# Attention heads unrolled across loop borders, three-pass scores in two mixers, and no staged queries

## The reference

```python
def _nsa(q, kc_raw, vc_raw, ks, vs, kw, vw, gates, ...):        # 8 heads, 2 key groups, HD = 64
    kc = _compress(kc_raw, pos_k, ck_w1, ck_w2)                 # 31 compressed keys
    vc = _compress(vc_raw, pos_v, cv_w1, cv_w2)
    ...
        s_c = jnp.einsum('bqghd,bngd->bghqn', qc, kc) * scale
        p_c, _ = _probs(s_c, cmp_end[None, :] <= t[:, None])
        o_c = jnp.einsum('bghqn,bngd->bqghd', p_c, vc)
        ...                                                     # o_s: selected blocks, o_w: window
        return gc[..., 0:1] * o_c + gc[..., 1:2] * o_s + gc[..., 2:3] * o_w

def _dilated_mixture(q, k, v): ...                              # 8 heads, HD = 64, one mask with weights
def _mla_mixer(...):                                            # 16 heads
        sc = (einsum('bqhd,bkhd->bhqk', qn, k_nope) + einsum('bqhr,bkr->bhqk', qr, k_rope)) * scale
        p, _ = _probs(sc, k_pos[None, :] <= t[:, None])
        return jnp.einsum('bhqk,bkhd->bqhd', p, v)

def _gqa(q, k, v):                                              # 8 heads of 128, 2 key groups, 768 keys
    s = jnp.einsum('bqkgd,bskd->bkgqs', q, k) * (ATTN_HEAD_DIM ** -0.5)
    p = jax.nn.softmax(s, axis=-1)
    return jnp.einsum('bkgqs,bskd->bqkgd', p, v)
```

## Time and profile before

| what | value |
|---|---|
| median of 3 runs | 3901.3 us (3901.02 to 3901.65) |
| profiled execution | 3896.48 us, its span 3894.7 us |
| PE busy | 3483.3 us (89%) |
| DVE busy | 2051.7 us (53%) |
| ACT busy | 1229.4 us (32%) |
| POOL busy | 271.5 us (7%) |
| chain that ended last | PE 77%, DVE 12%, ACT 3%, POOL 2% |
| share of the chain in `three` (L759 to L761) | 66% |
| compress stage, from 629.93 to 681.05 us | 51.12 us |
| `nsa` and `dil`, to 865.50 us | 184.45 us |
| `mla`, 1821.09 to 1938.50 us | 117.41 us |
| `attn`, 3292.74 to 3447.65 us | 154.91 us |

### The profile page before, as it was taken

How to read it: one execution, slowest core, us unless ns; L and a number is a source line. 1 busy time by engine, 2 the same in 40 slices (tenths; PEclk the granted TensorE clock), 3 DMA queues, 4 the chain that set the end, 5 groups by cost and what they waited for, 6 DMA issues and landing times.

```text
span 3894.7 us, 47690 instructions
## 1 busy us (share of the span) xinstructions
PE 3483.3 (89%) x16433; PEld 2822.0 (72%) x16433; DVE 2051.7 (53%) x2953; ACT 1229.4 (32%) x1890; POOL 271.5 (7%) x258
## 2 busy tenths in 40 slices
PE   8999988889999999988999994498899875778999
PEld 6888767567888788865678883398688753566887
DVE  7743433555753675355555435675655356335553
ACT  3222311443222322233532222454333232323332
POOL 1000111001000100022010003300000011000000
PEclk9999995999999999888999997599899987998999
DMA  5533240003542354211045420265233210012332
GB/s 170 171 94 98 88 109 1 0 7 112 168 124 81 109 171 124 81 59 33 1 118 167 124 92 27 59 172 163 76 97 102 91 65 22 1 43 76 97 103 70
DMA packets 390883, 347.27 MB, mean 89 GB/s; under 512 B 11344, under 2 KB 343437, under 8 KB 390669
## 3 DMA queue, kind: packets, MB, share of 16 engines
q1 hardware_dynamic: 390797, 346.16, 29.8%
HBM read 344.02 MB, written 2.10 MB: 89 GB/s over the span
## 4 chain that ended last, share of the span: by engine, by line
PE 77%; DVE 12%; issue 4%; ACT 3%; POOL 2%; SPq 1%; DMA 0%; DVEq 0%; ACTq 0%; POOLq 0%
PE ps L759 22%; PE ps L760 22%; PE ps L761 22%; PE ps L850 3%; PE ps L824 2%; POOL sq_sum L2147 2%; PE ps L1244 1%; ACT w_hi L1297 1%; DVE w_lo L1310 1%; DVE a_lo L1635 1%; DVE rstd L1658 1%; PE ps L841 1%; DVE x_T L2131 1%; PE ps L821 1%; PE ps L957 1%
## 5 line engine op out<-in xcount | busy, mean ns | idle before, releaser
L759 PE MATMUL ps<-a_hi,w_hi 128*128 128x512 f32 (+1 forms) x2968 | 1144.7, 386 | 135.5 <-DVE a_lo L1901 42.7
L760 PE MATMUL ps<-a_lo,w_hi 128*128 128x512 f32 (+1 forms) x2968 | 1130.6, 381 | 0.0
L761 PE MATMUL ps<-a_hi,w_lo 128*128 128x512 f32 (+1 forms) x2968 | 1130.0, 381 | 0.0
L759 PEld LDWEIGHTS ps<-a_hi,w_hi 128*128 128x128 f32 x2968 | 570.8, 192 | 281.4 <-issue 114.6
L1310 DVE TENSOR_TENSOR w_lo<-w_raw,w_hi 128x1024 fp32r<-128x1024 f32 (+1 forms) x536 | 636.3, 1215 | 183.3 <-ACT w_hi L1297 169.4
L1297 ACT ACTIVATE w_hi<-w_raw 128x1024 fp32r<-128x1024 f32 (+1 forms) x536 | 549.8, 1044 | 308.5 <-PE ps L761 306.7
L761 PEld LDWEIGHTS ps<-a_hi,w_lo 128*128 128x128 f32 x2968 | 571.6, 193 | 103.8
L760 PEld LDWEIGHTS ps<-a_lo,w_hi 128*128 128x128 f32 x2968 | 572.5, 193 | 100.8 <-issue 1.0
L759 PE MATMUL ps<-hs_hi,w_hi 128*128 128x512 f32 (+1 forms) x1232 | 464.9, 377 | 2.8 <-DVE w_lo L1310 1.5
L760 PE MATMUL ps<-hs_lo,w_hi 128*128 128x512 f32 (+1 forms) x1232 | 463.7, 376 | 0.0
L761 PE MATMUL ps<-hs_hi,w_lo 128*128 128x512 f32 (+1 forms) x1232 | 463.3, 376 | 0.0
(11 more groups left out here) (250 smaller groups left out, 3251.5 us busy)
## 6 DMA issues: line engine op xcount, KB each, us to landing
w_raw<-in_ffn_w_up SPq DMA_DIRECT2D x220, 512.0 KB, 4.8
w_raw<-in_ffn_w_down SPq DMA_DIRECT2D x154, 512.0 KB, 3.5
ada_raw<-in_ada_w SPq DMA_DIRECT2D x96, 512.0 KB, 3.9
w_raw<-in_ffn_w_gate SPq DMA_DIRECT2D x88, 512.0 KB, 5.1
w_raw<-in_ev_w_in SPq DMA_DIRECT2D x20, 512.0 KB, 3.6
w_raw<-in_attn_w_qkv SPq DMA_DIRECT2D x16, 512.0 KB, 4.2
w_raw<-in_ev_w_out SPq DMA_DIRECT2D x8, 512.0 KB, 4.1
w_raw<-in_mla_w_out SPq DMA_DIRECT2D x8, 512.0 KB, 3.2
```

The lines of the kernel that those rows point to most:

```text
L759: mm(dst, hi, rhi, start=start, stop=False)
L760: mm(dst, hi, rlo, start=False, stop=False)
L761: return mm(dst, lo, rhi, start=False, stop=stop)
```

## The change

1. **Unrolled units.** `attention` on PE, ACT and DVE walks all units in straight code. PE's order per unit u and step j is: scores(u+1, next tile), transposes(u, j+1), values(u, j), across the old iteration borders too. At the last step the first transpose of u+1 stands ahead of the last values of u.
2. **ACT's order.** A `take` of step j now stands ahead of the exponentials of unit u+1 that it stood between or behind: `attn` has take, exp instead of exp, take; the causal mixers have take 1, exp 0, exp 1, take 3, exp 2, exp 3.
3. **Scale.** The softmax scale, with its sign turned, is multiplied into the queries where they are made (and into the gains of `mla` and `attn`); the masks change sign, DVE takes minima, and the exponential has scale -1 and that minimum as its bias. L1690 and a wait between DVE and ACT go.
4. **No staging.** POOL's copies and the `stage` tiles go. Scores read queries and keys in place: 64 rows of `F` in `nsa` and `dil`, 96 in `mla`, 128 in `attn`.
5. **Three-pass scores** in `nsa`, `dil` and `attn`: ACT makes the high part of a 128x512 tile (`qk_hi`), DVE the rest (`qk_lo`). In the even mixer 14 tiles: 7 inside the rope loop, 7 (`later`) one in each of `nsa`'s units 0 to 6. In `attn` 10: 4 before the first unit, 6 one in each of units 0 to 5. On DVE `qk_lo` stands between the last maximum of u+1 and `finish(u)`. `mla` keeps one float32 matmul.
6. **Compress** has no loop: scores of two heads in one three-pass matmul of 64 columns (48 matmuls), softmax on 4 heads at a time (two groups of 128x512), 8 transposes, 8 float32 value matmuls of 256 columns with block-diagonal values.

The core of the diff:

```diff
+            ph.cmp.step0 = dve_step.plan(12)
+
+            def pair(f, rows):
+                return F_hi(f)[rows, :], F_r[rows, f, :]
+
+            def head(f_q, f_k, side, v, out, need, gate=None):
+                rows = slice(HD * side, HD * side + HD)
+                return dict(q=pair(f_q, rows), k=pair(f_k, rows), v=v, out=out, gate=gate, need=ph.qk0 + need)
+
+            heads = []
+            for it in range(4):
+                for branch in range(2):
+                    for side in range(2):
+                        gate = it * 3 + 12 * side + 1 + branch
+                        heads.append(head(it, 6 + 2 * branch, side,
+                                          lambda kb, b=branch, s=side: v_tok[:, kb, b, HD * s:HD * s + HD],
+                                          o_tok[:, :, it * HD + 256 * side:it * HD + 256 * side + HD], 6,
+                                          gates[:, :, gate:gate + 1]))
+            ph.nsa = attention_plan(heads, "causal", work=work_even, mask=masks[:, 0, :], dim=HD,
+                                    later=[[(F[:, f, :], F_hi(f), F_r[:, f, :])] for f in SPLIT[7:]])
...
+            splits, heads = [], []
+            for i in range(2):
+                splits.append((k_att[:, i, :], k_att_hi[:, i, :], k_att_lo[:, i, :]))
+                for u in range(4):
+                    h = 4 * i + u
+                    splits.append((q_att[:, h, :], q_att_hi[:, h, :], q_att_lo[:, h, :]))
+                    heads.append(dict(q=splits[-1][1:], k=splits[5 * i][1:], v=lambda kb, i=i: v_att[:, kb, i * P:i * P + P],
+                                      out=o_att[:, :, h * P:h * P + P], gate=None, need=ph.qk0 + len(splits)))
+            ph.first_splits = splits[0:4]
+            ph.att = attention_plan(heads, "full", work=work_att, mask=zeros[:, :], dim=P, later=[[x] for x in splits[4:]])
...
+                ring = 2 if full else 4
+                units_t = [(c, range(3 * h, 3 * h + 3)) for c in range(4) for h in range(2)] if full else \
+                    [(c, range(c + 1)) for c in range(4)]
+
+                def scores(u, c):
+                    head = at.heads[u]
+                    if c == 0 and head["need"] is not None:
+                        pe.wait_ge(qk_lo_s.sem, head["need"])
+                    if 4 * u + c >= ring:
+
+                        pe.wait_ge(sm_s.sem, at.sm0 + 4 * u + c - ring + 1)
+                    parts = [(0, 512, 2 * (c % 2)), (512, 768, 2 * (c % 2) + 1)] if full else [(0, (c + 1) * P, c)]
+                    for first, end, bank in parts:
+                        dst = ps[:, bank, 0:end - first]
+                        q = [t[:, c * P:(c + 1) * P] for t in head["q"]]
+                        k = [t[:, first:end] for t in head["k"]]
+                        if len(q) == 2:
+                            last = three(dst, q[0], q[1], k[0], k[1], True, True)
                         else:
-                            last = mm(ps[:, c, 0:(c + 1) * P], q, at.k(it, u, (c + 1) * P), start=True, stop=True)
...
+                def turn_(u, j):
+                    c, kbs = units_t[j]
...
+                def values(u, j):
+                    c, kbs = units_t[j]
+                    made, first = ((ptd_s, at.ptd0), (pta_s, at.pta0))[j % 2]
+                    pe.wait_ge(made.sem, first + per_t // 2 * u + j // 2 + 1)
+                    if j == 0 and u >= 2:
...
+                for c in range(4):
+                    scores(0, c)
+                for u in range(at.units):
+                    if u == 0:
+                        turn_(0, 0)
                     for j in range(per_t):
-
-                        if u < 3 and j % (per_t // 4) == 0:
-                            scores(u + 1, it, (j // (per_t // 4),))
+                        if u + 1 < at.units and j % (per_t // 4) == 0:
+                            scores(u + 1, j // (per_t // 4))
                         if j + 1 < per_t:
-                            turn_(j + 1)
...
-                with pe.Fori(0, at.units // 4) as it:
-                    scores(0, it)
-                    for u in range(4):
-                        rest(u, it)
...
+                    for it in range(4):
+                        for c in range(4):
+                            tok = slice(c * P, (c + 1) * P)
+                            dst = ps[:, it // 2, :].rearrange("p (i s c n) -> p i s c n", i=2, s=2, c=4)[:, it % 2, :, c, :]
+                            last = three(dst, F_hi(it)[:, tok], F_r[:, it, tok], kc_hi[:, :], kc_lo[:, :], True, True)
...
+            def qk_hi(split):
+                do(split[1], split[0], ACT.Copy).then_inc(qk_hi_s.sem, 1)
+
...
-                def rest(u, it):
-                    for j in range(per_t):
-                        if u < 3 and j % (per_t // 4) == 0 and j % 2 == 0:
-                            exps(u + 1, it, (j // (per_t // 4),))
-                        if j % 2 == 0:
-                            continue
-                        act.wait_ge(t_s.sem, v_at(at.t0 + per_t * u + j + 1, it, 4 * per_t))
-                        if j >= 2:
-                            act.wait_ge(pv_s.sem, v_at(at.pv0 + per_t * u + j - 1, it, 4 * per_t))
-                        width = 384 if full else (j + 1) * P
-                        do(wk.pT[:, 1, 0:width], ps[:, 5, 0:width], ACT.Copy).then_inc(pta_s.sem, 1)
-                        if u < 3 and not full:
...
+                for c in range(4):
+                    exps(0, c)
+                for u in range(at.units):
+                    more = u + 1 < at.units
+                    for j in range(1, per_t, 2):
+                        take(u, j)
+                        for c in ((j // 2,) if full else (j - 1, j)) if more else ():
+                            exps(u + 1, c)
+                    for split in at.later[u] if u < len(at.later) else ():
+                        qk_hi(split)
...
+            def qk_lo(split, n):
+                src, hi, lo = split
+                dve.wait_ge(qk_hi_s.sem, n + 1)
+                v.tensor_tensor(lo, src, hi.bitcast(F32), ALU.subtract).then_inc(qk_lo_s.sem, 1)
...
-                            v.tensor_scalar(NM[:, u % 2, c:c + 1], MX[:, u % 2, c:c + 1], -at.scale, None, ALU.mult)\
-                             .then_inc(nm_s.sem, 1)
...
+                for c in range(4):
+                    maxima(0, c)
+                for u in range(at.units):
+                    more = u + 1 < at.units
+                    for j in range(0, per_t, 2):
+                        take(u, j)
+                        for c in ((j // 2,) if full else (j, j + 1)) if more else ():
+                            maxima(u + 1, c)
+                    for split in at.later[u] if u < len(at.later) else ():
+                        qk_lo(split, split0 + nsplit[0])
+                        nsplit[0] += 1
+                    finish(u)
...
+                        if 3 <= r <= 9:
+                            f = ROPED[r - 2]
+                            qk_lo((F[:, f, :], F_hi(f), F_r[:, f, :]), ph.qk0 + r - 3)
...
-            def stage_queries(at):
-
-
-                stage = at.work.stage
-                with pool.Fori(0, at.units // 4) as it:
-                    for u in range(at.stages):
-                        q, side = at.q(it, u)
-                        rows = slice(0, at.rows) if side is None else slice(HD * side, HD * side + HD)
-
-                        pool.wait_ge(s_s.sem, v_at(at.s0 - 16 + 4 * (u + 1 if at.stages == 4 else u + 3), it, 16))
-                        g.tensor_copy(stage[rows, u, :].unsqueeze(1), q[rows]).then_inc(st_s.sem, 1)
```

505 lines of the change are left out of this document (244 added, 261 removed).

## The result

The changed kernel takes 3929.95 us (median of 4 runs, 3925.06 to 3935.03) against 3901.16 (3899.97 to 3901.65): a ratio of 1.0074, 95% interval 1.0057 to 1.0092, so 28.8 us slower. The profiled execution took 3930.02 us, 33.5 more than the one of before. Later executions of the kernel before took 3884 to 3927 us (3884 to 3907 in nine on one chip); none of them is traced, so which stage makes this spread isn't known.

What follows compares the result with a forecast made beforehand. PE, busy 89% of the span and holding 77% of the chain, was taken as the bound. Compress -23.6, attn -38, mla -12, nsa and dil +84, projection +2.3 gave +12.7: 3914 us on the median, range 3828 to 3930.

Steps and rivals of the forecast that it cites:

- nsa and dil: Stages nsa and dil: clock at 0.50 throughout, units of 12.2, 10.8 and 10.3 us, +84 us (+72 to +92).
- the term for mla: Stage mla: ACT's wait goes, units of 6.4 instead of 7.1 us, -12 us (-2 to -14).
- Rival 3: Low clock reaches mla too: five units stay there at 5.4 us more each, kernel 3941 us; chance 0.05.
- One of my own signs: Forecast is wrong if three passes of 512 columns on 64 rows take over 0.7 us at full clock.
- The start of nsa: nsa was to start at 1.2 GHz, since compress stays there.
- the sign of rival 1: Whether the clock comes up in nsa and dil is decided in the first 10 us of nsa.
- rival 1: Clock comes up in nsa and dil as now: 169 to 192 us there, kernel 3825 us; chance 0.18.
- the reason given: nsa and dil: the one thing in a unit after which the clock rose, 128-row float32 scores, is taken out.
- attn: Stage attn: take ahead of exp ends ACT's wait, tile 3.12 us, split waits 10 us in all; -38 us (-30 to -41).
- Compress: Stage compress: batched matmuls and softmax, 51.1 to 27.5 us, -23.6 us (-18 to -30).
- Projection: Output projection behind nsa and dil starts at 1.2 GHz, +2.3 us.
- the prediction's inference from that rule: nsa and dil: transposes don't raise the clock, so half clock is likelier still, with the same sum.

Runs made afterwards that it cites:

- 2: Changed kernel with the even mixer's 7 later splits made during compress's score matmuls instead of in nsa's units; 3898.36 us.
- 3: Changed kernel without splits in the even mixer: one float32 score matmul each, nsa and dil on 64 rows in place; 3911.12 us.
- 1: Changed kernel with nsa and dil scores contracting all 128 rows of the same tiles, so sums over two heads; 3823.17 us.
- 4: 3 with POOL copying nsa and dil queries to zero-padded tiles, so float32 scores contract 128 rows; 3793.73 us, 0.971 of the kernel before.
- 9: Changed kernel with DVE's first take of the next unit ahead of qk_lo and the output; 3794.80 us, five more executions 3769.75 to 3904.79.
- 10: 9 plus one long PE wait in nsa's seventh unit, with nsa and dil scores on 64 or 128 rows; 3879.94 and 3780.72 us.
- 12: Changed kernel with float32 scores everywhere, 128 rows in nsa, dil and mla, no attn splits, DVE's take first; 3752.93 us, 0.9645 of the kernel before.
- 7: Changed kernel with ACT making the next unit's exponential ahead of the take again in attn; 3962.99 us.

## Why the prediction was wrong

It said 3914, 12.7 us slower, and the kernel is 28.8 slower, 3929.95. That the number lies inside the range to 3930, by 0.05 us, is luck. The direction and the main cause, nsa and dil at the low clock, were right. The step that failed is the term for mla, -12: it was worked out at the fast clock, and mla ran its first four and a half units at 0.50.

- **mla**, -12: measured +4.6. These 16.6 us are about the whole miss of 16; the other errors and the 4.7 us between the profiled pair and the medians nearly cancel. The units are shorter, as forecast (at 1.00 they are 6.05 us, forecast 6.4), but for 54 us they ran at 0.50, a unit in 10.86. Rival 3 described just this, five units at 5.4 us more each (4.8 measured), and I gave it 0.05, with the argument that mla's scores are unchanged and the clock came up before. But it came up in a stage that starts low and whose scores have 96 rows, so it can come up or not: with the same instructions mla took 95.9 or 96.0 us in 2 and 3 and 117.6 in the changed kernel, 1 and 4. Why it stayed low in the changed kernel is open.
- **nsa and dil**, +84: measured +93.8 from first transpose on (180.0 to 273.8), less 2.3 at the start. The clock stayed at 0.50 as forecast, but units took 12.54, 11.50 and 11.33 us, not 12.2, 10.8 and 10.3. The missing item is the change of height. I priced the passes from rows in which passes of one height follow each other, and 9 and 10 show 1.1 us a unit on top, at the fast clock, for changing between 64 and 128 rows. One of my own signs said so: three passes of 512 columns on 64 rows take 0.89 us there (9, from the first pass to the next transpose), over the 0.7 that I had set, and 0.78 on 128 rows (10), so 0.11 of it is the height. At the fast clock too a unit with the new scores (6.35) is slower than one with the old ones in the same order (5.49 in 12).
- **The start of nsa**: I let it start at the low clock, and it started at the fast one: the clock came up during compress's new value matmuls, 5.77 us at 128 rows. It held for 11.4 us and fell in the first split wait, 2.35 us (forecast 2.4 to 3.5). So the sign of rival 1, that the first 10 us of nsa decide, would have pointed the wrong way. That the low clock then lasts was forecast from the earlier trace rows and shown in 10. Of the reason given, that the only thing after which it rose is taken out, half is wrong: it came up without any scores behind dil's last ones (10) and in the projection's transposes. The trace of before showed as much: its first 32 transposes start 0.21 us apart and end 0.11 apart. The 64-row scores keep it low; long 128-row scores aren't needed.
- **DVE's order**: that moving one take keeps the clock high in most executions (9), I hadn't seen. With rival 1 I had that clock, but held it for a matter of one rule, while the same program can show both.
- **attn**, -38: measured -41.5 with its start. ACT's order is 34.6 of it (7). Tile 3.12 forecast, 3.05 measured; split waits 1.7 each and 10 in all forecast, 1.26 to 1.75 each and 8.5 in all measured.
- **Compress**, -23.6: nsa starts 23.8 earlier. **Projection**, +2.3: measured +2.4.

With the measured sizes the sum is -23.8 + 91.5 + 2.4 + 4.6 + 1.4 - 42.9 + 0.3 = +33.5 for the profiled pair. The 4.7 us to the medians' difference are the profiled execution of before, which was that much below its median.

The Trainium skill, "TensorE: Matmul & The Clock Gate", "What's actually happening", says that activity releases the throttle. Here PE's being busy wasn't enough: in 2 it was busy for 254.26 of 256.00 us and stayed at 0.50, and with 128-row scores in the same places the clock came back within 6.8 us (10). The same page's "Part 4: PE-mode transpose" says that transposes don't raise the clock. The traces here don't agree, and the measurement decides. The first thing that PE does in the changed kernel, from 6.42 us on, is 32 float32 transposes; they start 0.21 us apart at first and 0.11 at the end (12 instructions in 2.58 us, then 22 in 2.60), so the clock rose on transposes alone. It came up in the same way behind dil, after 5.07 us of them, with value matmuls and a pause of 0.59 us ahead. So the prediction's inference from that rule, that half clock is likelier still, isn't borne out.

## What to carry to other kernels

A matmul that uses half the rows isn't only half empty: between short 128-row matmuls it can hold TensorE at 1.2 GHz to the end of the stage once the clock has dropped, at PE busy 99%. Padding with zeros to 128 rows then pays for its copies many times over (4). Look for the instruction that the next unit waits for and see what stands ahead of it on its engine without need: moving one copy ahead of the output was worth 135 us here in all but one execution, moving ACT's take ahead of its exponential 35. Where the clock rows of two kernels differ, read the clock stage by stage before explaining the difference with the edit.

## What I had not expected of the hardware

- Both clocks can last in one program: nsa with dil in 154.4 us at 1.00 or in 265.6 at 0.50, PE busy 98 to 99.8% of the time (9).
- The low clock ends with the 64-row scores: 198 us at 0.50, then 1.00 after 5.8 us of transposes and values (10).
- Transposes alone raise the clock: 32 in a row, 0.21 us apart at first and 0.11 at the end (start of the changed kernel).
- Changing between matmuls on 64 and on 128 rows costs 0.14 us each time: 6.35 us a unit against 5.22 for the same instructions, without a wait (9, 10).
- mla's first units at 0.50 or at 1.00, 117.6 or 95.9 us, in programs that don't differ there (4 and 2).
